# First layer's up-projection in seven products of halves: blocks 2 to 10, with the operand sums on GpSimd and the residual put aside

## The chip, the cores and the metric

The kernel runs on one core of one Trainium2 chip. Its time is device microseconds (us) for one execution. Five engines work side by side on their own instruction streams: TensorE (PE, matmuls into PSUM), VectorE (DVE), ScalarE (ACT), GpSimd (POOL) and SyncE (SP, which here issues transfers). They wait for each other through semaphores.

## The reference, cut to what matters

The model is two blocks; the second is a transformer of two layers, and the change lies in the feed-forward part of its first layer, where 512 latent and 256 context tokens (768 together) go through the same weights.

```python
def swiglu(h, w_i, w_o):
    g, u = jnp.split(h @ w_i, 2, axis=-1)
    return (jax.nn.silu(g) * u) @ w_o

# D_MODEL = 1024, FF_HIDDEN = 2816, DEPTH = 2
xl = xl + ml[5] * rms_norm(swiglu(adaln(xl, g[2], ml[3], ml[4]), w_ffn_in[l], w_ffn_out[l]), g[3])
if with_ctx:      # layer 0 only
    xc = xc + mc[5] * rms_norm(swiglu(adaln(xc, g[2], mc[3], mc[4]), w_ffn_in[l], w_ffn_out[l]), g[3])
```

## The kernel before

Every operand of a product is kept as a high part, rounded to the matmul's format, and a low part, the rest. A product is three matmuls: high with high, high with low, low with high. High parts are copies on ScalarE (line 182, `cvh`), low parts subtractions on VectorE (line 3202, `cvl`).

The hidden width of 2816 is worked off in 11 blocks of 256 gate and 256 up columns. The tokens stand in `HI` and `LO`, transposed, as 8 slices of 128 of the 1024 inner columns by 768 tokens. One block is three things:

- up: four chunks of two slices each; a chunk is 4 groups of columns x 2 slices x 3 matmuls, once for 512 tokens and once for 256. Sums of four groups by 768 tokens fill PSUM banks 0 to 5 (line 2241 records all matmuls).
- gate (`gated_ff`): for two groups of 128 columns and the two spans of tokens ScalarE takes silu of the gate sum into a ring of parts in `EX`, VectorE multiplies by the up sum out of PSUM (line 3208), ScalarE writes the high part into `AC`, and VectorE the low part (line 3213).
- down: `AC` times the block's 256 rows of the second weight, in two halves of 512 output columns and six tiles of 128 tokens, 6 matmuls of 512 columns a tile, into banks 6 and 7 in turn. VectorE adds each tile to the result in `AR` (line 3221; for block 0 it copies, line 3218), which frees the bank.

The weights come by transfers on SP (line 3319): 2 MB for a block's up part, as two of 1 MB, and 1 MB for its down part, each staged into `WR` when the low part of the last chunk before has been written. Converted chunks go through a ring of four (`WD` and three parts of `WC`, `wcr`), two results `AC` through a ring of two.

The order is written out in the planner: `P.add` appends a step, and each engine runs its part of the steps in that order and waits where a step names what it needs. In block b the up chunks come first, then one gate step, then the down tiles of block b-1, with one further gate step behind each of the first tiles (`next(gating, None)`) and conversions of the next chunks between. Behind block 10 `ending` adds the normed result to the residual `X` and `XC` (GpSimd, line 3276), norms it for the next layer (lines 2814, 2826, 2830, 2836, 3133), and the next layer's weights are converted. `x_spill` is a buffer in HBM to which the residual is written at an earlier place of each layer (line 3324). The line numbers of the profile are those of the kernel before.

Of the kernel before, what the change touches and what calls it, by code (L numbers as in the profile page):

```python
# [9 lines left out]
F32 = mybir.dt.float32  # L10
# [248 lines left out]
def build(nc, A, out, dump=None):  # L259
    with ExitStack() as ctx:  # L260
# [1160 lines left out]
        def rope(x, copied):  # L1421

            if P.count["rope_s"] == P.count["rope_g"]:
                P.add("rope_s", x, copied)
                return []
            return [("rope_d", 2 * P.add("rope_g", x, copied))]
# [217 lines left out]
        for l in range(2):  # L1644
# [515 lines left out]
            convert(*work[3])  # L2160
            next_at = [4]
# [4 lines left out]
            for kind, b, c in sched[2:]:  # L2166
                turns = () if kind == "act" else (0,) if kind == "up" or not both else ((), (0, 3))[c]
                if 0 in turns:
                    convert_next()
                if kind == "up":  # L2170
                    j, o, ready = conv.pop((kind, b, c))
                    up_n = up(c, o, [ready], [span_of(s_, th, lo, hi) for s_, (lo, hi) in enumerate(fspans)])
# [17 lines left out]
                elif c == 0:  # L2190

                    for _ in gating:
                        pass
                    halves = [conv.pop((kind, b, c_)) for c_ in range(2)]
                    ja, ac, an = staged["ac", b]
                    cols, cneed = scale_cols(CL[0:2], 1, 1, gcol(1, 0))
                    ths = [None] * 6

                    def ending(halves=halves, b=b, ja=ja, ac=ac, an=an, done={}, nu=tuple(x for b_ in (2, 3) for x in ufree[b_]), both=both, nt=nt, down=down,
                               Yf=Yf, GF=GF, fneed=fneed, yat=yat, JUNK=JUNK, hn1=hn1, cols=cols, cneed=cneed, ths=ths):  # L2200

                        for i in range(nt + 3):
                            if i < nt:
                                for c_, (j, o, ready) in enumerate(halves):
                                    down(i, c_, b, o, ready, ac, an)
                            if 1 <= i <= nt:
                                done[i - 1] = add_normed(Yf[:, i - 1, :], i - 1, GF, [*fneed, ("dn_d", yat[i - 1, 0]), ("dn_d", yat[i - 1, 1])], JUNK)
                                if not both:
                                    P.add("store", i - 1, done[i - 1])
                            if both and 2 <= i <= nt + 1:  # L2210
                                v = Norm(xt(i - 2), [HDs[1], (LTs if i < 6 else LXs)[1]], 128 * (i - 2), cols[(i - 2) // 4], modcol(1, 0, (i - 2) // 4), [cneed, done[i - 2]])
                                v.lo_col, v.tmps = 128 * ((i - 2) % 4), [AR[:, 21504 + 512 * c:22016 + 512 * c] for c in range(2)]
                                v.banks, v.until, v.hn = (2, 3), nu, hn1
                                norm_begin(v)
                                ths[i - 2] = v
                            if both and i >= 3:
                                ths[i - 3] = norm_end(ths[i - 3])
                            yield
                    follow = ending()
                    if both:  # L2220
                        w = load(A["w_in_2"][1][:, 2560:3072], 8, 512, 0)
                        wturn[0] = 1
                        next_weights = SplitWeights(w, 512, WR_AT, [(2, AR_AT + 4 * 22528), (2, AR_AT + 4 * 23552), (2, AR_AT + 4 * 26624), (2, AR_AT + 4 * 27648)],
                                                    acs.until[1 - ja])
                    for i in range(nt):
                        next(follow)
                        if both and i < 4:
                            next_weights.convert()
                    if not both:
                        for _ in follow:  # L2230
                            pass
                    if both:
                        order, tring_until = list(range(6)), [tuple(ufree[4]), tuple(ufree[5])]
                        lring_until = [tuple(ufree[0]), tuple(ufree[1]), drn.until[0], drn.until[1]]
# [5 lines left out]
        def pe_program(e):  # L2240
# [989 lines left out]
        def pool_program(e):  # L3230
# [47 lines left out]
            def rope_s(n, x, copied):  # L3278
                w = RTs[1][0:32, :].rearrange("p (g n) -> p g n", g=3)
                e.wait_all(copied)  # L3280
                e.wait_ge("rope_d", 2 * n - 2)
                for lo in (0, 16):
                    e.o.dma_start(w[lo:lo + 16, :, :], x[16 - lo:32 - lo, :, :]).then_inc(sem("rope_dm"), 16)

            def rope_g(n, x, copied):
# [4 lines left out]
                e.wait_ge("rope_d", 2 * n - 2)  # L3290
                tt(u, x, cc, ALU.mult)
                e.wait_ge("rope_dm", 32 * n)
                tt(w, w, ss, ALU.mult).then_inc(sem("rope_d"))
                e.wait_ge("rope_d", 2 * n - 1)
                tt(x, u, w, ALU.add).then_inc(sem("rope_d"))
# [104 lines left out]
```

## Time and profile before

| | |
|---|---|
| median of 3 runs | 3134.68 us (3126.94 to 3135.32) |
| profiled execution | 3128.29 us, span 3127.0 us |
| TensorE | 2854.2 us busy, 91% of the span |
| VectorE | 1583.7 us, 51% |
| ScalarE | 1020.1 us, 33% |
| GpSimd | 309.3 us, 10% |
| mean granted clock of TensorE | 0.965 |
| first layer's feed-forward | 1642 to 2216 us of the span |

The span goes from the first to the last instruction; the execution's own time is 1.3 us longer. The granted clock is a share of 2.4 GHz; the other level is 1.2 GHz (0.5). Matmul rows of a timeline overlap, since they are pipelined: the time that one takes from the next is the distance of their starts. "x72" in a row stands for 72 like instructions in a row. In brackets is the idle time of the engine before the instruction, and what ended it.

### The profile page before, as it was taken

What the parts mean: (1) busy time and instruction counts of PE and PEld (TensorE: products, weight loads), DVE (VectorE), ACT (ScalarE), POOL (GpSimd) and SP (SyncE); (2) the same over time, 40 slices, a digit from 0 to 9 for tenths busy, and PEclk for the clock granted to TensorE, in tenths of its full rate; (3) what the DMA queues carried; (4) which work ended last, traced back from release to release, by engine and by line L of the source; (5) the groups of instructions that cost most, each with busy time, mean ns of one, the idle gap of its engine ahead of it and who ended that gap; (6) DMA issues with size and microseconds to landing.
All of it is one profiled execution on the core that took longest, in us unless ns stands there. A gap on an engine that the chain in (4) does not pass through costs nothing.

```text
span 3127.0 us, 43494 instructions
## 1 busy us (share of the span) xinstructions
PE 2854.2 (91%) x18290; PEld 2314.0 (74%) x18290; DVE 1583.7 (51%) x3063; ACT 1020.1 (33%) x1974; POOL 309.3 (10%) x294
## 2 busy tenths in 40 slices
PE   7988889999999998898799999999899797899998
PEld 6767678877877666787568888888656686578886
DVE  4333534444445355777673433434835767654444
ACT  3223422332343255334232221212426443332222
POOL 0000022222200000100000000000201245000001
PEclk9999999999999999899899999999999898999999
DMA  6433342222222210323602212121121110223231
GB/s 230 158 111 130 108 104 66 66 66 66 74 93 111 46 34 1 105 69 102 218 13 95 68 55 70 52 81 65 44 46 34 38 35 11 85 95 120 82 108 54
DMA packets 228879, 250.96 MB, mean 80 GB/s; under 512 B 6048, under 2 KB 193548, under 8 KB 227404
## 3 DMA queue, kind: packets, MB, share of 16 engines
q1 hardware_dynamic: 227008, 243.87, 24.7%
q0 software_dynamic: 1344, 4.20, 0.6%
q8 instruction: 144, 2.36, 0.3%
q14 instruction: 51, 0.42, 0.0%
q10 hardware_dynamic: 332, 0.12, 0.0%
HBM read 234.53 MB, written 9.44 MB: 78 GB/s over the span
## 4 chain that ended last, share of the span: by engine, by line
PE 55%; DVE 9%; ACT 4%; issue 2%; DMA 1%; POOL 0%; SPq 0%; DVEq 0%; ACTq 0%; POOLq 0%
PE PS L2241 52%; PE PS L2245 2%; ACT AR L182 1%; DMA WR<-in_w_in 1%; ACT L177 1%; PE PS L2452 1%; DVE AR L3221 1%; DVE STAT L3153 1%; ACT EX L182 1%; DVE EX L3208 0%; DVE AR L2984 0%; DMA WR<-in_w_mod 0%; ACT STAT L182 0%; DVE AR L2968 0%; DVE OBl L3202 0%
## 5 line engine op out<-in xcount | busy, mean ns | idle before, releaser
L2241 PE MATMUL PS<-HI,WC 128*128 128x512 f32 (+2 forms) x1600 | 428.1, 353 | 0.6 <-DVE WC L3202 0.6
L2241 PE MATMUL PS<-AR 128*64 128x64 f32 (+7 forms) x3436 | 301.8, 267 | 58.8 <-ACT AR L182 25.5
L2241 PEld LDWEIGHTS PS<-AR 128*64 128x64 f32 (+5 forms) x3436 | 255.0, 169 | 110.5 <-issue 37.5
L182 ACT ACTIVATE AR<-PS 128x512 f32<-128x512 f32 (+5 forms) x353 | 152.1, 458 | 529.5 <-PE PS L2241 407.7
L2241 PEld LDWEIGHTS PS<-HI,WC 128*128 128x128 f32 x1600 | 284.0, 189 | 42.4 <-DVE WC L3202 1.1
L2241 PE MATMUL PS<-LO,WC 128*128 128x512 f32 (+2 forms) x800 | 282.2, 353 | 0.0
L2241 PE MATMUL PS<-HT,WR 128*128 128x256 f32 (+1 forms) x928 | 260.5, 434 | 8.4 <-DMA WR<-in_w_in 5.0
L2241 PE MATMUL PS<-WR,HT 128*128 128x128 f32 (+2 forms) x1296 | 254.2, 354 | 12.0 <-ACT AR L182 5.0
L182 ACT ACTIVATE EX<-PS 128x256 f32<-128x256 f32 (+2 forms) x158 | 66.5, 430 | 537.0 <-PE PS L2241 536.9
L2241 PEld LDWEIGHTS PS<-WR,HT 128*128 128x128 f32 x1296 | 193.6, 199 | 63.4 <-issue 39.8
L2241 PEld LDWEIGHTS PS<-HT,WR 128*128 128x128 f32 x928 | 174.4, 193 | 73.2 <-issue 45.1
L2241 PE MATMUL PS<-WC,AC 128*128 128x512 f32 x960 | 227.2, 393 | 0.3
L2241 PE MATMUL PS<-DH,DW 128*128 128x512 f32 x608 | 204.0, 404 | 9.5 <-DVE DW L3202 9.5
L2241 PEld LDWEIGHTS PS<-WC,AC 128*128 128x128 f32 x960 | 178.6, 189 | 43.9 <-DVE AR L3221 7.4
L3202 DVE TENSOR_TENSOR WC<-WR,WC 128x1024 fp32r<-128x1024 f32 x96 | 116.3, 1222 | 165.4 <-ACT WC L182 165.4
L182 ACT ACTIVATE WC<-WR 128x1024 fp32r<-128x1024 f32 x96 | 99.9, 1054 | 273.0 <-PE PS L2241 273.0
L2245 PE MATMUL PS<-CON,AR 128*128 128x128 f32 (+1 forms) x806 | 129.3, 288 | 56.8 <-DVE AR L3169 17.8
L3208 DVE TENSOR_TENSOR EX<-EX,PS 128x512 f32<-128x512 f32 x66 | 39.2, 594 | 256.7 <-ACT EX L182 256.7
L2245 PEld LDWEIGHTS PS<-CON,AR 128*128 128x128 f32 (+1 forms) x806 | 98.0, 147 | 94.1 <-issue 43.9
L2241 PEld LDWEIGHTS PS<-LO,WC 128*128 128x128 f32 x800 | 151.3, 189 | 20.4
L3221 DVE TENSOR_TENSOR AR<-AR,PS 128x512 f32<-128x512 f32 x200 | 134.7, 683 | 37.0 <-PE PS L2241 36.4
L2241 PE MATMUL PS<-DW,DH 128*128 128x384 f32 (+1 forms) x576 | 149.0, 342 | 3.3 <-DVE DW L3202 2.4
(461 smaller groups left out, 5249.9 us busy)
## 6 DMA issues: line engine op xcount, KB each, us to landing
WR<-in_w_ffn_in SPq DMA_DIRECT2D x40, 1024.0 KB, 6.7
WR<-in_w_in_b SPq DMA_DIRECT2D x51, 512.0 KB, 6.7
WR<-in_w_mod SPq DMA_DIRECT2D x12, 2048.0 KB, 8.0
WR<-in_w_mod SPq DMA_DIRECT2D x24, 1024.0 KB, 5.5
WR<-in_w_ffn_out SPq DMA_DIRECT2D x22, 1024.0 KB, 5.0
WR<-in_w_in SPq DMA_DIRECT2D x40, 512.0 KB, 5.2
WR<-in_w_out SPq DMA_DIRECT2D x8, 2048.0 KB, 10.8
WR<-in_w_in SPq DMA_DIRECT2D x4, 2048.0 KB, 8.0
```

The lines of the kernel that those rows point to most:

```text
L177: self.o.preload_act_table_set(need)
L182: return self.o.activation(out, in_, func, **kw)
L2241: mm = lambda o, l, r, start, stop: e.o.matmul(o, l, r, start=start, stop=stop, skip_group_check=True)
L2245: m = e.o.transpose(bk[0:a.shape[1], 128 * i:128 * i + a.shape[0]], a, ident[0:a.shape[0], 0:a.shape[0]])
L2452: m = e.o.matmul(o, q, k, start=True, stop=True)
L3153: e.o.tensor_reduce(st[:, m_:m_ + 1], a.from_[m_], AXY, ALU.max).then_inc(sem("df_v"))
L3202: tt(lo, src, hi.bitcast(F32), ALU.subtract).then_inc(sem("cv_d"))
L3208: tt(v, v, pu, ALU.mult).then_inc(sem("gt_m"))
L3221: tt(y, y, bk, ALU.add).then_inc(sem("dn_d"))
```

## The change

Blocks 2 to 10 of the first layer compute a block's up part in another form. The inner dimension is cut in halves of 512 and the tokens in halves of 384; for a pair p (128 gate columns with 128 up columns) the 2x2 product of halves is made of seven products in place of eight, by sums and differences of the operands ahead (weights: `weight_sums`, four of 128x512 a pair; tokens: `token_sums`, once for all blocks) and additions of the results behind (`rj`, VectorE, line 3426 after). Each product is 4 slices x 3 matmuls of 384 columns. Two pairs make 14 products in the order `ORDER7`. The operand sums run on GpSimd (`gsum`, line 3536 after, new). Weights are converted in chunks of two products (128x512 each, `convert_two`). The first, second and fifth product are copied from PSUM by ScalarE (128x384). The gates of the first pair run between products, those of the second pair between down tiles (`last_gates`). The space for the sums of the tokens is `X` and `XC`: the residual goes to HBM ahead of them (3 MB) and comes back in block 10, behind the last product, on SP ahead of the next layer's weights; `add_normed` waits for it. Blocks 0 and 1, and the second layer, keep their form.

```diff
+            def weight_sums(p):
+                a11, a12, a21, a22 = quarters_of(p)
+                s1 = gsum(Z1, a21, a22, ALU.add, staged["up"].ready, *zfree[0])
+                s3 = gsum(a21, a11, a21, ALU.subtract, s1)
+                s2 = gsum(Z2, Z1, a11, ALU.subtract, s3)
+                sums_ready[p] = gsum(Z4, a12, Z2, ALU.subtract, s2)
+            def token_sums():
+                P.add("ld", "spill", XSP[:, 0:4096], X, n, need)
+                P.add("ld", "spill", XSP[:, 4096:6144], XC, n, need)
...
+                p = gsum(x0, *b12, ALU.add, *free)
+                q = gsum(x1, *b11, ALU.add, p)
+                p = gsum(t1, x0, x1, ALU.subtract, q)
+                q = gsum(x1, *b22, ALU.add, p)
+                p = gsum(t2, x1, t1, ALU.subtract, q)
+                q = gsum(t3, x1, x0, ALU.subtract, p)
...
+                p = gsum(t4, *b21, ALU.add, ("up", up_n), q)
+                q = gsum(t4, t4, t2, ALU.subtract, p)
...
+            ORDER7 = [(0, 1), (0, 2), (0, 6), (0, 5), (0, 7), (1, 1), (1, 2), (0, 3), (0, 4), (1, 6), (1, 5), (1, 7), (1, 3), (1, 4)]
...
+                    first_copy(0, product(0))
+                    gate_first(0, product(1))
+                    convert_two(b, 4)
+                    second_copy(0, product(2))
+                    fifth_copy(0, product(3))
+                    convert_two(b, 5)
+                    up_second(0, product(4))
+                    first_copy(1, product(5))
+                    convert("down", b - 1, 0)
+                    gate_first(1, product(6))
+                    gate_second(0, product(7))
+                    convert_two(b, 6)
+                    pairs[0].n4 = product(8)
+                    gate(0, 0)
+                    second_copy(1, product(9))
+                    gate(0, 1)
+                    convert("down", b - 1, 1)
+                    fifth_copy(1, product(10))
+                    gates_end()
+                    up_second(1, product(11))
+                    down_tiles(b - 1, 0, range(2))
+                    gate_second(1, product(12))
+                    pairs[1].n4 = product(13)
+                    if b == 10:
+                        for to, lo, hi in ((X, 0, 4096), (XC, 4096, 6144)):
+                            P.add("ld", "spill", to, XSP[:, lo:hi], P.count["fence"], (("up", pairs[1].n4),))
+                    gate(1, 0)
+                    def last_gates():
+                        gate(1, 1)
+                        staged["ac", b] = ja, ac, gates_end()
+                    if b < 10:
+                        weight_sums(0)
+                        down_tiles(b - 1, 0, range(2, nt), {2: last_gates, 4: lambda: convert_two(b + 1, 0)})
+                        down_tiles(b - 1, 1, range(nt), {0: lambda: convert_two(b + 1, 1), 3: lambda: convert_two(b + 1, 2)})
+                        convert_two(b + 1, 3)
...
             def up(n, o, c, HH, need, spans):
                 e.wait_all(need)
+                if c is None:
+                    p, opens = spans
+                    for k in range(4):
+                        mm(p, o[:, 0, k, :], HH[0][k], opens and k == 0, False)
+                        mm(p, o[:, 0, k, :], HH[1][k], False, False)
+                        m = mm(p, o[:, 1, k, :], HH[0][k], False, k == 3)
+                    m.then_inc(sem("up"))
+                    return
...
+            def gsum(n, o, x, y, op, need):
+                e.wait_all(need)
+                tt(o, x, y, op).then_inc(sem("gp_sum"))
```

On VectorE, before, a stretch of down tiles in a steady block: line 3221 is the add of a down tile, 3208 a gate's multiplication, 3213 a gate's low part (`AC` is its result).

```order
L3208 TENSOR_TENSOR EX<-EX,PS 128x256 [waits s_gt_s]
L3221 TENSOR_TENSOR AR<-AR,PS 128x512 [waits s_dn_d,s_dn]
L3213 TENSOR_TENSOR AC_273<-EX,AC_273 128x256 [waits s_gt_h]
L3208 TENSOR_TENSOR EX<-EX,PS 128x512 [waits s_gt_s]
L3221 TENSOR_TENSOR AR<-AR,PS 128x512 [waits s_dn_d,s_dn]
L3213 TENSOR_TENSOR AC_273<-EX,AC_273 128x512 [waits s_gt_h]
L3208 TENSOR_TENSOR EX<-EX,PS 128x256 [waits s_gt_s]
L3221 TENSOR_TENSOR AR<-AR,PS 128x512 [waits s_dn_d,s_dn]
```

The same place after; 3458 is the add of a down tile, 3445 a gate's multiplication, 3450 a gate's low part, 3426 an addition of products.

```order
L3426 TENSOR_TENSOR EX<-EX,PS 128x384 [waits s_cv_a,s_up]
L3458 TENSOR_TENSOR AR<-AR,PS 128x512 [waits s_dn_d,s_dn] x2
L3426 TENSOR_TENSOR EX<-EX,PS 128x384 [waits s_up]
L3445 TENSOR_TENSOR EX<-EX,PS 128x384 [waits s_gt_s]
L3450 TENSOR_TENSOR AC_273<-EX,AC_273 128x384 [waits s_gt_h]
L3445 TENSOR_TENSOR EX<-EX 128x384 [waits s_gt_s]
L3450 TENSOR_TENSOR AC_273<-EX,AC_273 128x384 [waits s_gt_h]
L3458 TENSOR_TENSOR AR<-AR,PS 128x512 [waits s_dn_d,s_dn] x2
```

Before, one gate step stood between two adds; after, two whole gates stand between the second and the third add.

On GpSimd, before, nothing stands between the work on the mixer (line 3239) and the addition to the residual behind the feed-forward (line 3276).

```order
L3239 TENSOR_TENSOR AR<-X,AR 128x768 [waits s_hp_x,s_fence]
L3239 TENSOR_TENSOR AR<-X,AR 128x768 [waits s_hp_x]
L3239 TENSOR_TENSOR AR<-WR,AR 128x768 [waits s_hp_x] x2
L3239 TENSOR_TENSOR AR<-EX,AR 128x768 [waits s_hp_x] x2
L3276 TENSOR_TENSOR X<-X,AR 128x1024 [waits s_an_y,s_fence]
```

After, the sums (line 3536) follow there: six of the tokens, two more behind the up part of block 1, and then four of weights for each pair, of which the first four stand here.

```order
L3536 TENSOR_TENSOR X<-HI_270,LO_271 128x1536 [waits s_spill,s_cv_d,s_norm_l,s_pj,s_norm_h,s_fence]
L3536 TENSOR_TENSOR X<-HI_270,LO_271 128x1536 [waits s_gp_sum]
L3536 TENSOR_TENSOR XC<-X 128x1536 [waits s_gp_sum]
L3536 TENSOR_TENSOR X<-HI_270,LO_271 128x1536 [waits s_gp_sum]
L3536 TENSOR_TENSOR WR<-X,XC 128x1536 [waits s_gp_sum]
L3536 TENSOR_TENSOR AR<-X 128x1536 [waits s_gp_sum]
L3536 TENSOR_TENSOR AR<-HI_270,LO_271 128x4x384 [waits s_gp_sum,s_up]
L3536 TENSOR_TENSOR AR<-AR,WR 128x4x384 [waits s_gp_sum]
L3536 TENSOR_TENSOR WR<-WR 128x512 [waits s_w0]
L3536 TENSOR_TENSOR WR<-WR 128x4x128 [waits s_gp_sum]
L3536 TENSOR_TENSOR XC<-WR 128x512 [waits s_gp_sum]
L3536 TENSOR_TENSOR AR<-WR,XC 128x512 [waits s_gp_sum]
```

Each sum waits for the one before it; the two operands of a sum lie in SBUF.

## Rows read from the trace of the kernel before

**Rows 1.** The page: busy us by engine; the chain of waits by line.

```profile
PE 2854.2 (91%) x18290; PEld 2314.0 (74%) x18290; DVE 1583.7 (51%) x3063; ACT 1020.1 (33%) x1974; POOL 309.3 (10%) x294
...
PE PS L2241 52%; PE PS L2245 2%; ACT AR L182 1%; DMA WR<-in_w_in 1%; ACT L177 1%; PE PS L2452 1%; DVE AR L3221 1%; DVE STAT L3153 1%; ACT EX L182 1%; DVE EX L3208 0%; DVE AR L2984 0%; DMA WR<-in_w_mod 0%; ACT STAT L182 0%; DVE AR L2968 0%; DVE OBl L3202 0%
```

**Rows 2.** Stretches: us, busy PE, PEld, DVE, ACT, POOL; granted clock, DMA share, GB/s.

```profile
1936.16:1986.45 50.29, 50.23 (x265) 42.73 (x264) 18.64 (x26) 9.87 (x14) 0.00 (x0) 1.00 0.20 63
...
2200.00:2220.00 20.00, 14.19 (x57) 10.93 (x58) 19.42 (x23) 9.31 (x21) 5.66 (x2) 0.83 0.00 1
1676.00:1686.00 10.00, 7.94 (x46) 6.87 (x45) 2.88 (x6) 4.60 (x8) 0.00 (x0) 1.00 0.01 2
```

**Rows 3.** TensorE's timeline in a steady block: start us, length us, engine, line, operation.

```profile
1959.81 0.62 PE L2241 MATMUL PS<-HI,WC 128*128 128x512 f32 x2
...
1960.49 0.62 PE L2241 MATMUL PS<-HI,WC 128*128 128x512 f32 x2
...
1966.31 17.12 PE L2241 MATMUL PS<-WC,AC 128*128 128x512 f32 x72
1983.27 0.39 PE L2241 MATMUL PS<-HI,WD 128*128 128x512 f32 x1
...
1991.60 0.40 PE L2241 MATMUL PS<-HI,WC 128*128 128x512 f32 x1
```

**Rows 4.** TensorE's timeline where matmuls of 384 columns stand.

```profile
390.55 0.51 PE L2241 MATMUL PS<-DW,DH 128*128 128x384 f32 x2
...
391.58 0.51 PE L2241 MATMUL PS<-DW,DH 128*128 128x384 f32 x2
```

**Rows 5.** Groups by form: count, busy us, mean ns of one, idle before.

```profile
L3221 DVE TENSOR_TENSOR AR<-AR,PS 128x512 f32<-128x512 f32 x200 | 134.7, 683 | 37.0 <-PE PS L2241 36.4
...
L3295 POOL TENSOR_TENSOR AR<-AR 32x1536 f32<-32x1536 f32 x12 | 41.6, 3468 | 0.9
...
L182 ACT ACTIVATE AR<-PS 128x384 f32<-128x384 f32 x36 | 17.6, 488 | 69.3 <-PE PS L2241 67.0 <-PE PS L2245 2.2
...
L2996 DVE TENSOR_TENSOR AR<-AR 128x384 f32<-128x384 f32 x27 | 15.1, 560 | 0.9
...
L3272 POOL TENSOR_TENSOR AR<-AR 96x512 f32<-96x512 f32 x4 | 5.2, 1322 | 266.7 <-ACT AR L182 266.7
```

**Rows 6.** Timeline of all engines where GpSimd and VectorE meet.

```profile
2203.57 2.83 POOL L3276 TENSOR_TENSOR X<-X,AR 128x1024 f32<-128x1024 f32 x1 [4.16 <-DVE AR L3133]
...
2204.07 0.68 DVE L2826 TENSOR_TENSOR AR<-PS,MISC 128x512 f32<-128x512 f32 x1
...
2204.78 2.16 DVE L2830 TENSOR_TENSOR AR<-AR,MOD 128x512 f32<-128x512 f32 x1
...
2207.58 0.69 DVE L2830 TENSOR_TENSOR AR<-AR,MOD 128x512 f32<-128x512 f32 x1
```

**Rows 7.** VectorE's timeline in the down tiles of a steady block.

```profile
1967.90 0.69 DVE L3221 TENSOR_TENSOR AR<-AR,PS 128x512 f32<-128x512 f32 x1
1968.52 0.69 DVE L3213 TENSOR_TENSOR AC<-EX,AC 128x512 fp32r<-128x512 f32 x1
...
1973.31 0.42 DVE L3213 TENSOR_TENSOR AC<-EX,AC 128x256 fp32r<-128x256 f32 x1
```

**Rows 8.** TensorE's timeline at the first product of block 1.

```profile
1681.35 0.47 PE L2241 MATMUL PS<-HI,WD 128*128 128x512 f32 x1 [2.06 <-ACT EX L182]
```

**Rows 9.** Transfers, issue to landing: feed-forward weights; residual; next layer's weights.

```profile
DMA to landing us min/median/max: 4.8/5.2/8.3
...
DMA to landing us min/median/max: 13.4/13.4/13.4
...
DMA to landing us min/median/max: 5.0/8.1/10.0
```

**Rows 10.** TensorE's last down product, and the first use of the next weights.

```profile
2167.51 3.82 PE L2241 MATMUL PS<-WC,AC 128*128 128x512 f32 x16
...
2184.74 1.06 ACT L182 ACTIVATE SW2h<-WR 128x1024 fp32r<-128x1024 f32 x1 [8.39 <-PE PS L2241]
```

More of the change, by code:

```diff
@@ L1425, in rope @@
                 return []
-            return [("rope_d", 2 * P.add("rope_g", x, copied))]
+            return [("gp_sum", 2 * P.add("rope_g", x, copied))]
         def head_project(h):
@@ new lines, in weight_sums, with convert_two @@
+            def weight_sums(p):
[4 more added lines that the diff above has]
+                sums_ready[p] = gsum(Z4, a12, Z2, ALU.subtract, s2)
+            def convert_two(b, x):
+                j, wc, until = wcr.take()
+                for half, (p, m) in enumerate(ORDER7[2 * x:2 * x + 2]):
+                    a11, a12, a21, a22 = quarters_of(p)
+                    src = {1: a11, 2: a12, 3: Z4, 4: a22, 5: Z1, 6: Z2, 7: a21}[m]
+                    o = wc[:, 1024 * half:1024 * half + 1024].rearrange("p (s k n) -> p s k n", s=2, k=4)
+                    n = P.add("cvh", o[:, 0], src, staged["up"].ready if m in (1, 2, 4) else sums_ready[p], until)
+                    n = P.add("cvl", o[:, 0], o[:, 1], src, n)
+                    unit[p, m] = o, ("cv_d", n)
+                chunk_at[x] = j
+                zfree[0] = (("cv_d", n),)
+                if x == 3:
+                    weight_sums(1)
+                if x == 6:
+                    wuntil[0] = zfree[0]
+                    if b < 10:
+                        stage_w("up", b + 1)
@@ new lines, in down_tiles @@
+            def down_tiles(b, c, tiles, hooks=()):
+                j, o, ready = conv["down", b, c]
+                ja, ac, an = staged["ac", b]
+                hooks = dict(hooks)
+                for i in tiles:
+                    if i in hooks:
+                        hooks[i]()
+                    down(i, c, b, o, ready, ac, an)
+                    next(gating, None)
+                if i == nt - 1:
+                    conv.pop(("down", b, c))
+                    wcr.done(j, ("dn", yat[i, c]))
+                    if c == 1:
+                        acs.done(ja, ("dn", yat[i, c]))
@@ L2161, in build @@
+            sums = token_sums() if both else iter(())
+            next(sums, None)
             next_at = [4]
@@ L2166, in build @@
             for kind, b, c in sched[2:]:
+                if both and kind == "down" and b == 0:
+                    break
                 turns = () if kind == "act" else (0,) if kind == "up" or not both else ((), (0, 3))[c]
@@ L2171, in build @@
                     j, o, ready = conv.pop((kind, b, c))
+                    if both and b == 1 and c:
+                        next(sums)
                     up_n = up(c, o, [ready], [span_of(s_, th, lo, hi) for s_, (lo, hi) in enumerate(fspans)])
@@ L2189, in build @@
                         acs.done(ja, ("dn", yat[nt - 1, c]))
[L2190 to L2234, printed above, removed]
@@ new lines, in build @@
+            follow = ending()
+            if both:
+                w = load(A["w_in_2"][1][:, 2560:3072], 8, 512, 0)
+                wturn[0] = 1
+                next_weights = SplitWeights(w, 512, WR_AT, [(2, AR_AT + 4 * 22528), (2, AR_AT + 4 * 23552), (2, AR_AT + 4 * 26624), (2, AR_AT + 4 * 27648)],
+                                            acs.until[1 - ja])
+            for i in range(nt):
+                next(follow)
+                if both and i < 4:
+                    next_weights.convert()
@@ L2235, in build @@
+            if not both:
+                for _ in follow:
+                    pass
+            if both:
+                order, tring_until = list(range(6)), [tuple(ufree[4]), tuple(ufree[5])]
+                lring_until = [tuple(ufree[0]), tuple(ufree[1]), drn.until[0], drn.until[1]]
             dump_now(f"z{l}", X)
```

156 lines of the change are left out of this document (150 added, 6 removed).

## The prediction, made before the change was run

> **What bounds the kernel now.** I read the page first, for which engine fills the span: TensorE is busy 91% of it, and the line that records its matmuls is 52% of the chain of waits [rows 1]. The line is a helper's, so it says nothing of the place; the table by stretches does [rows 2]. In the part that the change touches a block of the feed-forward takes 50.3 us, and TensorE is busy 50.2 of them at a granted clock of 1.00, VectorE 18.6, ScalarE 9.9, GpSimd nothing. So inside a block every column taken from TensorE is time, as long as the others, with 30 us of room, keep their order. The third view is TensorE's timeline, for what a column costs there [rows 3]: three matmuls of 512 columns start in 0.68 us, 0.227 each; an up chunk (24 of 512 and 24 of 256) goes from 1983.27 to 1991.60, 8.33; the 72 of the down product from 1966.31 to 1983.27, 16.96, against 72 x 0.227 = 16.3, so twelve tiles with waits that are all but met cost 0.6 together. The last two views are the durations by form on the three other engines [rows 5] and a stretch where GpSimd and VectorE work at once [rows 6].
>
> **Columns.** Before, a block's up-projection is 4 x 8.33 = 33.3 us. After, it is 14 products of 12 matmuls of 384 columns. This trace has that shape elsewhere: 6 start in 1.03 us [rows 4], so 12 in 2.06; I take 2.08 for a product with its wait met, 29.1 for a block. That is 4.2 less, 38 over nine blocks. The rest of the working is what this leaves.
>
> **The gate chain between the down tiles (+2.0 a block).** Before, the eight gate steps are spread, one behind each down tile: an add at 1967.90, a low part right behind it, the last low part at 1973.31 [rows 7], and TensorE never waits. After, both gates of the second pair stand on VectorE between the add of tile 1 and that of tile 2 of the first down half. There are two banks for down tiles, so tile 4 waits for tile 2's add. From the last product's end: ScalarE's copy through silu 0.5, with 0.3 until it starts; multiplication 0.55; high part 0.5; low part and second multiplication about 0.5 each; second high part 0.5; low part 0.5; the add 0.68; with rows of 0.49 (384 from PSUM), 0.56 (384, VectorE) and 0.68 [rows 5] that is about 4.9 (estimate). Tiles 2 and 3 fill 2.7 + 0.2. Left: 2.0. Bounds 1.0 to 2.8.
>
> **The second copy (+0.5 a block).** The second pair's weight sums start when the block's first chunks are converted (two high and two low parts at 0.55, 2.2 us into the block) and are four in a row on GpSimd: 1.32 for 512 elements [rows 5], 0.08 between, 5.5, with one collision of 0.4. ScalarE's conversion that needs the second of them (0.6) stands ahead of the copy (0.5) for which the fifth product waits. 2.2 + 5.5 + 0.4 + 0.6 + 0.5 = 9.2, less the parts of the chain behind that sum (0.2), against four products, 8.3 + 0.2. I take 0.5; bounds 0 and 1.1. The Trainium skill ("GPSIMD Engine Reference", "3.1 Elementwise — side-by-side cycle accounting") gives 4497 ns for an addition of 2048 elements; by an estimate from that page 512 take 1.12 us, this wait goes, and the sum is 4.5 lower. The row of 1.32 decides; no row here has 2048.
>
> **Twelve waits more (+0.3 a block).** Fourteen products in place of four chunks wait for weights, copies and banks; by 0.6 over twelve tiles above, some 0.03 to 0.05 each for ten. Bounds 0 and 0.6.
>
> Steady sum: -4.2 + 2.0 + 0.5 + 0.3 = -1.4, and nine times that -12.6.
>
> **The start (+13).** The sums of the tokens run on GpSimd while VectorE finishes the gates of block 0 and works through the down product of block 0. How the two share is the point on which this part rests [rows 6]. GpSimd's addition starts at 2203.57 and ends 2206.40. VectorE's addition with an input from PSUM, started inside it, takes its 0.68. Its next one, with both inputs in SBUF, starts at 2204.78 and takes 2.16, to 2206.94; the same line takes 0.69 at 2207.58. So a VectorE operation with two SBUF operands stands until GpSimd's instruction is over. Every low part, of conversions and of gates, is of this kind; multiplications with PSUM and the down adds are not. The Trainium skill has it as a rule ("SBUF — State Buffer", "Who interferes with whom"): an exclusive lock on a shared port pair, which whoever starts first holds for its whole instruction, and which a tensor_tensor with one input from PSUM does not need. The trace agrees (2.16 against 0.69, and 0.68 unmoved).
>
> A sum of 1536 elements a partition is 3.47 us [rows 5]. Six stand in a row in the first two blocks. The third and fourth gates of block 0, for whose banks the next product waits, have low parts ahead of them; two of these meet a sum, and I put 2.0 each, a bit over half of 3.5: +4.0 at a place where TensorE already waits 2.06 [rows 8]. Bounds 0 and 7.
> In the down product of block 0 GpSimd has two more of 3.5 and four of 1.3, 12.2 in all. VectorE has there 12 copies out of the banks (0.6 from start to start [rows 7], 7.2), block 1's gates (four multiplications and four low parts, half of them of 512 and half of 256, 3.8), six low parts of 512 (3.6) and two of 1536 (three times 0.6 each, 3.6): 18.2 against 16.3 of TensorE. With half of GpSimd's 12.2 as blocked time it is 24.2; 7.9 over, and 1.5 where the gates go to and fro with ScalarE: +9.4. Bounds 2 (no blocking) and 15 (all of it).
> Waits of 2 us and more can be followed by the lower level of the clock: the stretch from 2200, with waits of that size, had a granted clock of 0.83 on the mean, that from 1676, with the gap of 2.06 [rows 8], had 1.00 [rows 2]. At 0.83 of 20 us, 6.8 us ran at half (1.2 of 2.4 GHz), which is two falls of 3.4; a fall loses 1.7, since its matmuls take twice as long. The start has several such waits close together and I put one fall: +1.7, bounds 0 and 5.
>
> **The tail (+2).** The residual comes back by a transfer queued on SP ahead of the next layer's 2 MB of weights. Such a transfer landed 13.4 us after its issue, and the 2 MB 10.0 after theirs [rows 9]. Before, ScalarE uses these weights at 2184.74, 17.2 after the down product's start at 2167.51 [rows 10]. After, with the 2.0 above, it wants them 19.2 us after that start, and 13.4 + 10.0 is 23.4 if they run one behind the other, 19 to 22 if they share. Its work for the first add stands behind that. I take 2; bounds 0 and 6. The way out at the start (3 MB, behind two weight loads) is awaited by the first sum only; behind it on SP stand loads that are not due for another 30 us.
>
> **Sum.** -12.6 + 4.0 + 9.4 + 1.7 + 2 = +4.5. The profiled execution took 3128.3 (span 3127.0) and would take 3132.8; the median of the runs shown, 3134.7, is 6.4 above it, so 3139. The bounds add up to far more than is likely together (the gate chain 9 down and 7 up, the second copy 4.5 and 5.4, the waits 2.7 each way, the start 11 and 9, the clock 2 and 3, the tail 2 and 4; they have little to do with each other): the square root of the sum of squares is 15 each way. So this case goes from 3124 to 3154.
>
> **Rivals.**
> *The sums meet the gates in every block (slower).* The next block's up weights are issued when the last chunk of the current ones is converted: eight products (16.6), the waits (0.8) and the conversion (2.2), 19.6 us into a block. They land 8.3 later at the worst [rows 9], and the first pair's sums take 5.5: done at 33.4. The first low part of the second pair's gates is at 29.1 + 0.8 + 2.7 (two down tiles) + 1.9 (silu, multiplication, high part) = 34.5. From 1.1 us of delay on, by a transfer that meets another or by sums of over 1.6, every block has its two low parts blocked by up to 1.3 each, and the down adds that free the banks stand behind them: some 2.3 x 9 = 21, 3160. For it: 1.1 us is little beside landings between 4.8 and 8.3. Against: 8.3 is already the latest, 5.2 the median.
> *The clock falls in every block (slower).* A wait of 2 us comes once a block; 9 x 1.7 = 15, 3154. For it: 0.83 in the stretch from 2200. Against: 1.00 in that from 1676.
> *GpSimd does not hold VectorE up (faster).* Then the two terms of the start are 0 and 3.3, the fall of the clock goes, and 0.4 in each second copy: about -12.6 - 3.6 + 3.3 + 2 = -11, 3124. Against it stand [rows 6].
> *The waits are hidden (faster).* If TensorE finds other work or the gate chain is 2 us shorter, the steady sum is -3.9 a block, -35, and with the start, the clock and the tail 17 up: -18, 3117. For it: 30 us of room on VectorE [rows 2]. Against: TensorE takes its work in order, and the chain is a row of six steps of which none is under 0.4.
>
> **Chances.** My case 0.57, sums against gates 0.13, clock 0.12, no blocking 0.10, waits hidden 0.08. A measurement of this kernel can tell about 0.3%, 9.4 us, from no change, so faster is under 3125.3 and slower over 3144.1. My case gives 0.05 faster, 0.38 same, 0.14 slower; sums against gates 0.13 slower; clock 0.10 slower, 0.02 same; no blocking 0.05 and 0.05; waits hidden 0.08 faster. Together 0.18, 0.45, 0.37. The range, 3118 to 3161, leaves out the waits hidden and half of the case of sums against gates, and the edges of the others.
>
> **What would show it.** In the profile after: 12 matmuls of 384 start in about 2.06; a steady block takes 48.9; TensorE's idle time has 2 us for VectorE's down add once a block and about 0.5 for ScalarE's copy; VectorE's low parts have a mean well above 0.69 in the first down product alone; the stretch from the first product of block 0 to the end of block 0's down product is 13 longer. I am wrong if steady blocks have low parts of 1.5 or more, if the granted clock in them is under 0.97, if the first sums don't lengthen VectorE's work, or if a block's TensorE idle time is under 1 us.

## The result, and the profile after

The changed kernel takes 3142.3 us in the median of 11 runs (3138.6 to 3149.9), the kernel before 3128.0 in 11 (3122.9 to 3135.3). The ratio is 1.0047, 95% interval 1.0036 to 1.0058: slower by half a per cent, 14 us. The profiled execution took 3140.6, with a span of 3139.3, 12.3 over that of before.

Stretch by stretch, from the starts of TensorE's matmuls in the two traces (us):

| stretch | before | after | difference | forecast |
|---|---|---|---|---|
| up to block 0's second chunk | 1651.1 | 1655.6 | +4.5 | 0 |
| up parts of blocks 0 and 1 from there | 63.7 | 67.4 | +3.7 | +4.0 |
| down product of block 0 | 17.0 | 27.6 | +10.6 | +11.1 with the clock |
| nine blocks, from block 2's up part to block 10's down part | 452.7 | 449.0 | -3.8 | -12.6 |
| block 10's down part | 31.5 | 31.9 | +0.4 | +2 |
| the rest | 911.0 | 907.8 | -3.2 | 0 |

The first and the last line do not belong to the change. The first comes from a wait for a transfer of modulation weights 110 us earlier; over eight traces of these kernels, whose work there is the same, that stretch ended between 1645.7 and 1660.2, and the rest was shorter where it was late, so that the two add up to 2558 to 2564. What does it was not looked into. The line in which forecast and measurement part is the fourth. This is the table by stretches for four steady blocks, its columns as in [rows 2]:

```profile
1770.31:1819.34 49.03, 46.54 (x242) 42.38 (x241) 27.69 (x42) 16.12 (x30) 10.69 (x8) 1.00 0.19 65
1819.34:1869.71 50.37, 47.92 (x242) 43.62 (x241) 27.70 (x42) 16.12 (x30) 10.67 (x8) 0.97 0.19 63
1869.71:1918.71 49.00, 46.55 (x242) 42.40 (x241) 27.65 (x42) 16.12 (x30) 10.68 (x8) 1.00 0.19 65
1918.71:1969.31 50.60, 48.15 (x242) 43.58 (x241) 27.71 (x42) 16.12 (x30) 10.68 (x8) 0.97 0.19 63
```

and this the row of the nine blocks together:

```profile
1750.56:2199.54 448.98, 426.57 (x2161) 387.49 (x2160) 247.89 (x374) 143.84 (x266) 90.86 (x68) 0.98 0.21 74
```

A block has one of two lengths. At a clock of 1.00 it takes 49.0, 1.3 less than the 50.3 of [rows 2]; at 0.97 it takes 50.6, and the saving is gone. The same 242 matmuls are busy 1.6 us longer there (48.15 against 46.54): a fall of the clock, some 3.4 us at half. Five of the nine blocks (50.4 to 50.7 from start to start) have such a stretch, 5 x 1.6 = 8 us; the other four take 49.0.

Where TensorE waits in a steady block (its timeline; in brackets the wait and what ended it):

```profile
1783.39 2.92 PE L2470 MATMUL PS<-WD,AC 128*128 128x512 f32 x12
1788.12 3.02 PE L2470 MATMUL PS<-WD,AC 128*128 128x512 f32 x12 [1.80 <-DVE AR L3458]
...
1808.76 0.41 PE L2470 MATMUL PS<-T3h,WC 128*128 128x384 f32 x1 [0.68 <-ACT EX L182]
```

And what VectorE does meanwhile:

```profile
1784.14 0.56 DVE L3445 TENSOR_TENSOR EX<-EX,PS 128x384 f32<-128x384 f32 x1 [2.08 <-ACT EX L182]
1785.29 0.56 DVE L3450 TENSOR_TENSOR AC<-EX,AC 128x384 fp32r<-128x384 f32 x1 [0.59 <-ACT AC L182]
1785.77 0.55 DVE L3445 TENSOR_TENSOR EX<-EX 128x384 f32<-128x384 f32 x1
1786.90 0.56 DVE L3450 TENSOR_TENSOR AC<-EX,AC 128x384 fp32r<-128x384 f32 x1 [0.59 <-ACT AC L182]
1787.38 1.28 DVE L3458 TENSOR_TENSOR AR<-AR,PS 128x512 f32<-128x512 f32 x2
```

Tiles 2 and 3 run at 1783.39; tile 4 stands until 1788.12 for the add that VectorE reaches only behind the two gates, at 1787.38. VectorE is itself idle in between: it waits 0.59 twice for ScalarE's high part. The kernel before had an add behind each gate step there [rows 7]. The wait of 0.68 is the fifth product's, for the second copy.

At the start GpSimd's sums and VectorE's low parts meet. GpSimd's timeline, then VectorE's:

```profile
1687.17 4.00 POOL L3536 TENSOR_TENSOR XC<-X 128x1536 f32<-128x1536 f32 x1
1691.25 3.54 POOL L3536 TENSOR_TENSOR X<-HI,LO 128x1536 f32<-128x1536 f32 x1
```

```profile
1688.64 2.81 DVE L3450 TENSOR_TENSOR AC<-EX,AC 128x256 fp32r<-128x256 f32 x1 [0.48 <-ACT AC L182]
1691.38 0.67 DVE L3445 TENSOR_TENSOR EX<-EX,PS 128x512 f32<-128x512 f32 x1
1692.75 2.59 DVE L3450 TENSOR_TENSOR AC<-EX,AC 128x512 fp32r<-128x512 f32 x1 [0.70 <-ACT AC L182]
1695.27 0.41 DVE L3445 TENSOR_TENSOR EX<-EX,PS 128x256 f32<-128x256 f32 x1
```

A low part of 256 elements takes 2.81, to 1691.45, 0.3 behind the end of the sum of 1687.17; the next, of 512, takes 2.59, to 1695.34, 0.5 behind the end of the next sum. The multiplications between, with an operand in PSUM, take their usual 0.67 and 0.41. As in [rows 6], only the kind with two SBUF operands waits. TensorE's waits that follow:

```profile
1692.11 0.50 PE L2470 MATMUL PS<-HI,WD 128*128 128x512 f32 x1 [1.89 <-DVE EX L3445]
1695.73 0.39 PE L2470 MATMUL PS<-HI,WD 128*128 128x256 f32 x1 [1.24 <-DVE EX L3445]
...
1728.30 1.66 PE L2470 MATMUL PS<-WD,AC 128*128 128x512 f32 x6 [1.02 <-DVE AR L3455]
1732.18 2.41 PE L2470 MATMUL PS<-WD,AC 128*128 128x512 f32 x6 [2.22 <-DVE AR L3455]
1734.95 2.24 PE L2470 MATMUL PS<-WD,AC 128*128 128x512 f32 x6 [0.36 <-DVE AR L3455]
1738.42 5.70 PE L2470 MATMUL PS<-WC,AC 128*128 128x512 f32 x24 [1.23 <-DVE AR L3455]
1746.12 4.60 PE L2470 MATMUL PS<-WC,AC 128*128 128x512 f32 x12 [2.00 <-DVE AR L3455]
```

These are 3.1 in block 1's up part and 6.8 in block 0's down product. The rows with 2.24 to 2.41 for six matmuls, against some 1.5, and the one with 4.60 for twelve, against 2.92 above, have matmuls at half the clock: it fell twice in this product, whose granted clock is 0.88 on the mean.

### The profile page after: what moved, and what is told of

Same layout as the page of the kernel before. It is cut to its first block, busy times and chain, and to the rows that moved or that the text cites. A ratio compares the mean times of both kernels' runs of the same rounds, so it can differ in the third digit from the quotient of the medians.

```text
span 3139.3 us, 43589 instructions
## 1 busy us (share of the span) xinstructions
PE 2834.7 (90%) x18074; PEld 2321.2 (74%) x18074; DVE 1686.3 (54%) x3212; ACT 1082.0 (34%) x2123; POOL 435.2 (14%) x374
## 4 chain that ended last, share of the span: by engine, by line
PE 67%; DVE 11%; ACT 5%; issue 2%; DMA 1%; POOL 1%; SPq 0%; DVEq 0%; ACTq 0%
PE PS L2470 63%; PE PS L2474 3%; ACT AR L182 1%; ACT L177 1%; DVE DW L3439 1%; PE PS L2659 1%; ACT EX L182 1%; PE PS L2681 1%; DMA WR<-in_w_in 1%; DVE STAT L3390 1%; DVE AC L3450 1%; DVE AR L3458 0%; DVE AR L3221 0%; DVE EX L3445 0%; DMA WR<-in_w_mod 0%
## 5 line engine op out<-in xcount | busy, mean ns | idle before, releaser
L2470 PE MATMUL PS<-HI,WC 128*128 128x512 f32 (+2 forms) x1176 | 330.6, 358 | 0.6 <-DVE WC L3439 0.6
L2470 PEld LDWEIGHTS PS<-HI,WC 128*128 128x128 f32 x1176 | 214.4, 188 | 25.5 <-DVE WC L3439 1.1
L182 ACT ACTIVATE EX<-PS 128x384 f32<-128x384 f32 (+3 forms) x176 | 75.4, 437 | 449.0 <-PE PS L2470 449.0
L2470 PEld LDWEIGHTS PS<-WC,AC 128*128 128x128 f32 x924 | 177.7, 195 | 65.4 <-DVE AR L3458 24.5
L2470 PE MATMUL PS<-LO,WC 128*128 128x512 f32 (+3 forms) x588 | 210.4, 358 | 0.0
L3439 DVE TENSOR_TENSOR WC<-WR,WC 128x1024 fp32r<-128x1024 f32 (+1 forms) x136 | 139.5, 1042 | 85.0 <-ACT WC L182 84.2
L182 ACT ACTIVATE WC<-WR 128x1024 fp32r<-128x1024 f32 (+1 forms) x136 | 110.8, 838 | 159.1 <-PE PS L2470 159.1
L2470 PEld LDWEIGHTS PS<-DH,DW 128*128 128x128 f32 x608 | 115.6, 190 | 37.0 <-DVE DW L3439 10.8
L3439 DVE TENSOR_TENSOR DW<-WR,DW 128x768 fp32r<-128x768 f32 (+1 forms) x84 | 92.4, 1122 | 83.7 <-ACT DW L182 83.6
```

The costliest lines, as they stand in the source:

```text
L182: return self.o.activation(out, in_, func, **kw)
L2470: mm = lambda o, l, r, start, stop: e.o.matmul(o, l, r, start=start, stop=stop, skip_group_check=True)
L3439: tt(lo, src, hi.bitcast(F32), ALU.subtract).then_inc(sem("cv_d"))
```

## The experiments

Each was timed in five rounds beside the kernel before, whose median was 3129.2 in the first four and 3128.8 in the last two, against 3128.0 above; so a time here compares with the changed kernel's 3142.3 to about 1 us. Line numbers of the variants differ from the changed kernel's by a few.

**The gate steps spread over the down tiles.** The second pair's gates go back between the adds, in nine blocks:

```diff
                     def last_gates():
-                        gate(1, 1)
                         staged["ac", b] = ja, ac, gates_end()
...
-                        down_tiles(b - 1, 0, range(2, nt), {2: last_gates, 4: lambda: convert_two(b + 1, 0)})
+                        down_tiles(b - 1, 0, range(2, nt), {3: lambda: gate(1, 1), 4: lambda: (last_gates(), convert_two(b + 1, 0))})
...
```

> Edit: the second pair's two gates no longer stand in a row on VectorE between the adds of down tiles 1 and 2; one gate step follows each of the down tiles 2, 3 (as in the kernel before). Theory (the row of gates makes TensorE wait 1.8 us at down tile 4 in each of nine blocks, and in about five of them this wait lets the clock fall for 3.4 us, 1.6 us each): the wait of 1.8 is gone or under 0.5, the granted clock is 1.00 in every steady block, a block takes 47.3 to 47.7, and the time is 9 x 1.4 to 1.8 and 5 x 1.6 less than the 3142 of the changed kernel: 3118 to 3122, below the 3128 of the kernel before. Rival (the wait only moves to another place, since the chain of six steps between ScalarE and VectorE is as long as ever): 3138 to 3142.

Measured: 3121.6 (3114.0 to 3126.4), ratio 0.9963 (0.9949 to 0.9978) to the kernel before. A steady block by stretches, and TensorE's timeline:

```profile
1797.00:1844.60 47.60, 46.23 (x242) 42.47 (x241) 27.58 (x42) 16.12 (x30) 10.65 (x9) 1.00 0.20 67
```

```profile
1778.41 5.64 PE L2469 MATMUL PS<-WD,AC 128*128 128x512 f32 x24
1784.77 1.40 PE L2469 MATMUL PS<-WC,AC 128*128 128x512 f32 x5 [0.72 <-DVE AR L3457]
```

Four tiles now run without a wait where it was 1.80, the steady blocks take 47.6 (the last 47.8), and none has a clock under 1.00. Of what the rival says 0.72 is true: a wait of this size appears two tiles later, behind the low parts of the next weights. The theory holds, for the wait (a block is 1.4 shorter than the changed kernel's 49.0) and for the clock, and one edit of the order puts the changed kernel ahead of the kernel before.

**Matmuls that nobody reads in the wait.** TensorE gets seven matmuls behind tile 3 of each of the nine blocks:

```diff
-                        down_tiles(b - 1, 0, range(2, nt), {2: last_gates, 4: lambda: convert_two(b + 1, 0)})
+                        down_tiles(b - 1, 0, range(2, nt), {2: last_gates, 4: lambda: (fill(), convert_two(b + 1, 0))})
...
+            def fill(n, o, ac, need):
+                e.wait_all(need)
+                for k in range(7):
+                    mm(PS[:, 0, 0:512], ac[:, 0, 0, 0:128], o[:, 0, 0, :], k == 0, k == 6)
...
```

> Edit: seven matmuls of 512 columns, whose result nobody reads, are put into TensorE's wait at down tile 4 (into a PSUM bank that is free there); 7 x 0.227 = 1.6 us, less than the wait of 1.8. Theory (the waits let the clock fall): the order of all else and the 1.8 us between tile 3 and tile 4 stay, the granted clock is 1.00 in every steady block, and the five blocks of 50.6 take 49.0: 3142 - 8 = 3134. Rival (the falls come from something else in these blocks): still several blocks at 0.97, 3140 to 3144. Second rival (the added matmuls are themselves in the way): every block longer, over 3144.

Measured: 3132.6 (3126.5 to 3136.4), ratio 1.0007 (0.9998 to 1.0017). A block and the nine blocks by stretches, and the place in TensorE's timeline:

```profile
1854.40:1903.40 49.00, 48.13 (x249) 43.69 (x248) 27.64 (x43) 16.12 (x30) 10.66 (x8) 1.00 0.19 65
1754.42:2195.93 441.51, 433.19 (x2224) 393.48 (x2223) 247.89 (x374) 143.87 (x266) 90.89 (x68) 1.00 0.21 73
```

```profile
1836.40 4.51 PE L2473 MATMUL PS<-WC,AC 128*128 128x512 f32 x19
1841.13 5.05 PE L2473 MATMUL PS<-WC,AC 128*128 128x512 f32 x21 [0.22 <-DVE AR L3466]
```

The first row of the timeline is tiles 2 and 3 with the seven added matmuls (12 + 7); tile 4 still starts 4.7 us behind tile 2, as in the changed kernel. So the chain is as long as it was, and yet no steady block is at 0.97, all take 49.0 to 49.2, and 9.7 us are gone (7.5 between the nine blocks of the two traces). So the falls of the clock come with TensorE's idle time at this place, and cost about 8 us. It is the cleanest of the runs: more work, less time.

**The second copy first.**

```diff
+                    second_copy(0, product(2))
                     convert_two(b, 4)
-                    second_copy(0, product(2))
```

> Edit: on ScalarE the second copy out of PSUM goes ahead of the conversions of the fifth weight chunk, one of which waits for GpSimd's sums. Theory (the fifth product waits for a copy that stands behind a conversion that waits for GpSimd): the wait of 0.66 us in front of the fifth product goes, 9 x 0.5 to 0.66 = 5 to 6 us: 3136 to 3137. Rival (the copy is late by itself, or the conversions pushed back make a later product wait): 3141 to 3145.

Measured: 3128.6 (3121.4 to 3137.0), ratio 0.9999 (0.9987 to 1.0010), 14 less than the changed kernel and more than either theory said. ScalarE's timeline in the changed kernel, then in this one, and TensorE's at tile 4:

```profile
1807.60 0.63 ACT L182 ACTIVATE WC<-XC 128x512 fp32r<-128x512 f32 x1 [3.02 <-POOL AR L3536]
1808.14 0.85 ACT L182 ACTIVATE EX<-PS 128x384 f32<-128x384 f32 x2
```

```profile
1807.25 0.49 ACT L182 ACTIVATE EX<-PS 128x384 f32<-128x384 f32 x1 [3.67 <-PE PS L2470]
1807.64 0.62 ACT L182 ACTIVATE WC<-WR 128x512 fp32r<-128x512 f32 x1
```

```profile
1789.32 3.04 PE L2470 MATMUL PS<-WD,AC 128*128 128x512 f32 x12 [1.80 <-DVE AR L3458]
```

The copy no longer stands behind the conversion that waits for GpSimd, and the fifth product's wait is gone. Blocks take 48.1 in place of 49.0: 0.65 of wait and 0.2 besides, 9 x 0.87 = 8. The other 6 or so are the clock: with the wait of 1.80 at tile 4 still there, only one of nine blocks has a fall (49.5), against five. Which of these waits is followed by a fall thus depends on more than its length; what decides it was not tried.

**The start.** The way out of the residual ahead of block 1's weights, the first weight sums ahead of the last two token sums, and these behind block 1's gates:

```diff
+            if both:
+                n, need = P.count["fence"], (("norm_s", P.count["norm2"]),)
+                P.add("ld", "spill", XSP[:, 0:4096], X, n, need)
+                P.add("ld", "spill", XSP[:, 4096:6144], XC, n, need)
+                spilled[0] += 32
             convert(*work[3])
...
-                p = gsum(t4, *b21, ALU.add, ("up", up_n), q)
+                p = gsum(t4, *b21, ALU.add, ("up", up_n), ("gt_l", P.count["gt"] + 3), q)
...
+                weight_sums(0)
                 next(sums)
-                weight_sums(0)
```

> Edit, blocks 0 and 1 alone: the residual's way out is issued ahead of block 1's weights, so that the six token sums start some 10 us earlier; the first weight sums go ahead of the last two token sums on GpSimd, and these wait until block 1's gates are done. The same sums are computed. Theory (VectorE's low parts wait for GpSimd's instruction while one runs, whole): no low part of the gates of blocks 0 and 1 meets a sum, their 2.6 to 2.8 us fall to 0.4 to 0.7, the waits of 1.9 and 1.2 us in block 1's up part go, those in the first down product shrink by half or more, and the time is 4 to 9 us less: 3133 to 3138. Rival (the start is long because VectorE has more to do there and goes to and fro with ScalarE): low parts shorter but TensorE's waits as before, 3140 to 3144.

Measured: 3133.8 (3128.7 to 3144.5), ratio 1.0016 (1.0004 to 1.0028). The up parts of blocks 0 and 1 take 63.7, as before the change, and the gates' low parts are at their usual length. They are told by the groups by form, the changed kernel first:

```profile
L3450 DVE TENSOR_TENSOR AC<-EX,AC 128x512 fp32r<-128x512 f32 x26 | 22.3, 857 | 3.9 <-ACT AC L182 2.8
...
L3450 DVE TENSOR_TENSOR AC<-EX,AC 128x256 fp32r<-128x256 f32 x4 | 9.0, 2239 | 1.0 <-ACT AC L182 1.0
```

```profile
L3451 DVE TENSOR_TENSOR AC<-EX,AC 128x512 fp32r<-128x512 f32 x26 | 17.9, 689 | 3.9 <-ACT AC L182 2.8
L3451 DVE TENSOR_TENSOR AC<-EX,AC 128x256 fp32r<-128x256 f32 x4 | 1.7, 420 | 1.0 <-ACT AC L182 1.0
```

The first down product still takes 26.4: what meets the sums now is something else. Timelines of VectorE and GpSimd, and TensorE's wait:

```profile
1716.89 4.54 DVE L3440 TENSOR_TENSOR WC<-WR,WC 128x512 fp32r<-128x512 f32 x2
1716.96 3.91 POOL L3537 TENSOR_TENSOR AR<-HI,LO 128x1536 f32<-128x1536 f32 x1 [16.11 <-DVE AC L3451]
...
1721.35 1.27 DVE L3456 COPY AR<-PS 128x512 f32<-128x512 f32 x2
1722.17 7.37 PE L2471 MATMUL PS<-WC,AC 128*128 128x512 f32 x24 [3.97 <-DVE AR L3456]
```

The first row is two low parts of block 2's weights, which nobody needs yet: the first takes 0.69, the second stands until the sum is over, and the copies that free PSUM, which would not wait by themselves, stand behind it on VectorE. The theory holds for the up parts. At the down product what it expected did not come: the waits were to shrink by half or more and went from 6.8 to 5.8 (3.97 and a later 1.82), since the wait for GpSimd only passed to the next instructions of its kind.

**The weight sums late.** The opposite: in steady blocks the sums are made to meet the gates.

```diff
-            def weight_sums(p):
+            def weight_sums(p, *more):
                 a11, a12, a21, a22 = quarters_of(p)
-                s1 = gsum(Z1, a21, a22, ALU.add, staged["up"].ready, *zfree[0])
+                s1 = gsum(Z1, a21, a22, ALU.add, staged["up"].ready, *zfree[0], *more)
...
-                        weight_sums(0)
+                        weight_sums(0, ("up", pairs[1].n4))
```

> Edit: in each steady block the first pair's weight sums for the next block wait for the current block's last product, so that they start 4 us later than in the changed kernel and run while the second pair's gates do. Nothing else is moved. Theory (a VectorE instruction with both operands in SBUF waits for the whole of the GpSimd instruction that it meets, in a steady block too): the two low parts of the second pair's gates grow from 0.56 to 1.3 or more each, TensorE's wait at down tile 4 from 1.8 to 3 to 4.5, a block is 1.2 to 2.7 longer, and the clock falls in more of the blocks: 3142 + 11 to 24, and up to 7 more for the clock, 3153 to 3173. Rival (sums of 512 elements are too short to matter, or the clash cost only at the start, with sums of 1536): within 3 us of 3142.

Measured: 3171.8 (3169.8 to 3184.3), ratio 1.0147 (1.0126 to 1.0168). TensorE's wait at tile 4, VectorE's timeline just ahead of it, and VectorE's groups by form:

```profile
1846.44 13.92 PE L2470 MATMUL PS<-WC,AC 128*128 128x512 f32 x48 [4.22 <-DVE AR L3458]
```

```profile
1841.20 1.51 DVE L3450 TENSOR_TENSOR AC<-EX,AC 128x384 fp32r<-128x384 f32 x1 [0.59 <-ACT AC L182]
1842.64 1.61 DVE L3445 TENSOR_TENSOR EX<-EX 128x384 f32<-128x384 f32 x1
1844.83 0.95 DVE L3450 TENSOR_TENSOR AC<-EX,AC 128x384 fp32r<-128x384 f32 x1 [0.59 <-ACT AC L182]
```

```profile
L3450 DVE TENSOR_TENSOR AC<-EX,AC 128x384 fp32r<-128x384 f32 x36 | 30.8, 856 | 31.5 <-ACT AC L182 31.5
...
L3445 DVE TENSOR_TENSOR EX<-EX 128x384 f32<-128x384 f32 x18 | 18.4, 1022 | 0.0
...
L3445 DVE TENSOR_TENSOR EX<-EX,PS 128x384 f32<-128x384 f32 x18 | 10.0, 554 | 24.9 <-ACT EX L182 24.9
```

The wait is 4.2 in place of 1.8, the eight blocks with the late sums take 52.9 to 53.9, and every one of them has a fall of the clock. Two low parts and a multiplication, each 0.55 or so in the changed kernel, take 1.51, 1.61 and 0.95 beside sums of 1.3 to 1.5; together they are 2.4 longer, which is what the wait has grown by. The last two rows of the groups are the same multiplication on one line: with both operands in SBUF it takes 1.02 on the mean (half of the 18 belong to the first pair, away from these sums), with one in PSUM 0.55. The Trainium skill ("SBUF — State Buffer", "Who interferes with whom") says that a VectorE instruction with two SBUF inputs contends with a GpSimd instruction that reads SBUF, and that one with at most one SBUF input, outside its 2-port modes, does not. The trace agrees (1.61 and 0.55).

**All of it together.** The edits of the first, third and fourth experiment, with the next weights' low parts one tile later, and block 2's conversions behind the sums:

```diff
...
-                down_tiles(0, 0, range(nt), {4: lambda: convert_two(2, 0)})
-                down_tiles(0, 1, range(nt), {0: lambda: convert_two(2, 1), 2: lambda: next(sums), 3: lambda: convert_two(2, 2)})
+                down_tiles(0, 0, range(nt))
+                down_tiles(0, 1, range(nt), {3: lambda: convert_two(2, 0), 4: lambda: next(sums), 5: lambda: convert_two(2, 1)})
+                convert_two(2, 2)
                 convert_two(2, 3)
...
-                        down_tiles(b - 1, 0, range(2, nt), {2: last_gates, 4: lambda: convert_two(b + 1, 0)})
+                        down_tiles(b - 1, 0, range(2, nt), {3: lambda: gate(1, 1), 4: last_gates, 5: lambda: convert_two(b + 1, 0)})
...
```

> Edit: the gate steps spread over the down tiles with the next weights' low parts behind tile 4's add, the second copy ahead of the conversions, the residual's way out and the first weight sums earlier, the last two token sums behind block 1's gates, and in the first down product the conversions for block 2 behind the sums. All of the change is kept. Theory (the waits are separate and add up): blocks of 46.6 to 47.0 at a clock of 1.00, no wait over 2 us in the first down product; 3142 less 9 x 2.2 to 2.4 (gates and copy), less 8 (clock) and less 8 to 14 (start): 3100 to 3114, below the 3129 of the kernel before. Rival (what is taken away in one place comes back in the next, since VectorE's low parts and ScalarE's copies are as many): not under 3118.

Measured: 3094.4 (3089.6 to 3103.1), ratio 0.9897 (0.9875 to 0.9918): 34 us faster than the kernel before, 48 than the changed one, and 6 below the range that I had put. A block by stretches, and the first down product in TensorE's timeline:

```profile
1788.00:1834.30 46.30, 46.17 (x242) 42.40 (x241) 26.29 (x42) 16.24 (x30) 10.33 (x8) 1.00 0.21 69
```

```profile
1723.90 8.81 PE L2471 MATMUL PS<-WD,AC 128*128 128x512 f32 x36
1732.54 6.97 PE L2471 MATMUL PS<-WC,AC 128*128 128x512 f32 x30
1740.36 1.66 PE L2471 MATMUL PS<-WC,AC 128*128 128x512 f32 x6 [0.85 <-DVE AR L3456]
```

TensorE is busy 46.2 of 46.3 us again, as it was 50.2 of 50.3 before the change; the 4.0 between are the columns. The start costs 1.0 (81.7 against 80.6 for the up parts of blocks 0 and 1 and the first down product), where it was 14.3. The rival falls: the waits are separate, and do not come back. The two edits that are new here (the low parts a tile later, block 2's conversions later) were not run alone.

## Why the prediction came out as it did

The time was right, 3139 put and 3142 come, and so was the direction; the size of the change was not. I had reckoned +4.5, and it was +14.2 in the medians and +12.3 in the profiled executions. That the time came out even so is luck: the median of before, from which I set out, was 3134.7 in three runs and is 3128.0 in eleven, and this error hides two thirds of the other. Of the 12.3, 1.3 lie in the two stretches that the change does not touch; the start cost 14.3 where I had 15.1, the steady blocks gave 3.8 where I had 12.6, and the tail cost 0.4 where I had 2. The likeliest single outcome in my chances was no measurable change (0.45), and slower, which came, had 0.37.

- **Columns.** Right: two products start within 4.18 us (1750.56 to 1754.74 in the trace after), 2.09 each, where I took 2.08.
- **Gate chain.** Right: 1.8 in every block against 2.0, at the tile and behind the add that I had named. The sum had a slip: its parts add up to 4.5, or to 4.7 with the lengths of the rows, and not to the 4.9 that I put; the trace has 4.73 (1783.39 to 1788.12).
- **Second copy.** Right: 0.65 to 0.68 against 0.5.
- **Steady block.** Right without the clock: 49.0, 1.3 less than before, where I had 1.4 less. The other waits come to about 0.5 (49.0 less 29.1, 17.0, 1.8 and 0.65), not 0.3.
- **Start.** Right in place, cause and size: 3.7 and 10.6 where I had 4.0 and 9.4 + 1.7. In the first two experiments, whose start is the same code, the clock did not fall in the first down product, and it took 26.4: 9.5 more than before, against my 9.4. The two falls of the changed kernel add 1.1 to that, where I had 1.7 for one: its waits there come to 6.8, in those runs to 8.2. For the up parts the closeness is partly luck. Over the five traces that share this code the whole stretch took 94.1 to 98.7 us: the first sum, which waits for the residual's way out, starts 24.5 and 24.9 behind block 0's second chunk in two of them, and the up parts take 67.4 and 67.6; in the other three it starts at 23.1 to 24.1, and they take 69.7 to 71.6, with a fall of the clock.
- **The clock.** Here the step failed. I let it fall once, at the start, and kept the falls in the steady blocks as a rival with a chance of 0.12. It fell twice in the first down product and in five of nine steady blocks. The price in a steady block was right (1.6 against 1.7 a fall), the count was not: 8 us, which is nearly all of the difference between -12.6 and -3.8. I had weighed one gap without a fall [rows 8] against one stretch with two [rows 2], and took the first for the rule. My sign of being wrong, a granted clock under 0.97 in the steady blocks, could not tell either, since a block with one fall reads 0.97. A wait that comes back in every block at the same place should have had its own term, bounded by none and by nine falls.
- **Tail.** +0.4, not +2. ScalarE's first conversion of the next weights waited for TensorE and not for the transfer (its timeline after); I had run the two transfers one behind the other, or nearly so, and put the landing 19 to 23.4 behind the first issue; in the trace the residual's 3 MB and the first 1 MB of these weights were issued from 2181.81 to 2182.68 and had landed by 2198.35, 16.5 behind the first issue and 1.4 ahead of this row:

```profile
2199.80 1.06 ACT L182 ACTIVATE SW2h<-WR 128x1024 fp32r<-128x1024 f32 x1 [7.75 <-PE PS L2470]
```

- **Sums against gates in every block.** Did not happen, but by less than I thought. In the block shown above the first pair's sums end at 1784.75 and the first low part of the second pair's gates starts at 1785.29, half a microsecond to spare where I had 1.1. Over the eight blocks with such sums the spare is 1.3 to 1.5 in three, some 0.55 in two, and nothing in three (0.04 to -0.13), since the second half of the weights landed 7.7 to 9.2 after its issue and not 8.3 at the worst. This is the closest, GpSimd's row and then VectorE's:

```profile
1932.52 1.31 POOL L3536 TENSOR_TENSOR AR<-WR,XC 128x512 f32<-128x512 f32 x1
```

```profile
1933.70 0.56 DVE L3450 TENSOR_TENSOR AC<-EX,AC 128x384 fp32r<-128x384 f32 x1 [0.59 <-ACT AC L182]
```

The low part starts as the last sum ends and still takes its 0.56, as all 36 do on the mean. So in three blocks it was by luck that this rival did not come true. The late sums show what lay beyond: 2.4 more of wait a block, where I had put 2.3, and 3172 us, over the 3160 of that rival, since the clock falls in every block as well.
- **No blocking.** Refuted by the low parts at the start and by the late sums. **Waits hidden.** Not in this kernel; it took three edits of the order in the steady blocks to hide them (the gates, the copy, and the next weights' low parts a tile later).

## What to carry to other kernels

Taking work from the engine that is full pays only as far as the others keep pace in their order: 38 us of columns were taken here (an estimate from 9 x 4.2), and in the steady blocks 34 of them were lost to waits of under 2 us and to the clock that falls behind them; waits of up to 2.2 us at the start took the rest and 10 more. Before a new engine gets a share of the work, look which instructions of the others it blocks, and what stands behind these on a queue that goes in order; moving a dozen lines turned 14 us of loss into 34 of gain. A wait that comes back in every block has to be priced with the falls of the clock that may follow it.

## What the runs showed of the hardware that I had not expected

A wait of 1.8 us on TensorE, with one of 0.7 elsewhere in a block of 49, was followed by some 3.4 us at 1.2 GHz in five of nine blocks; with seven added matmuls in the same wait in none. In a block of 48.1 the same wait of 1.8 was followed by a fall in one of nine. And a VectorE low part of 256 elements, 0.42 us by itself, took 2.24 on the mean of four beside sums of 1.6 to 4.0 on GpSimd.
